# One hybrid decoder layer on one core: three products of TensorE move within the token mixer's step

## What is computed

```python
m = jnp.where(strict, jnp.einsum("bnhid,bnhjd->bnhij", k_beta, k) * decay, 0.0)
sol = lax.linalg.triangular_solve(m, rhs, left_side=True, lower=True, unit_diagonal=True)
attn_intra = jnp.einsum("bnhid,bnhjd->bnhij", q, k) * decay
...
v_new = u_i - jnp.einsum("bhck,bhkv->bhcv", w_i, state)
o = jnp.einsum("bhck,bhkv->bhcv", q_i, state) + jnp.einsum("bhij,bhjv->bhiv", a_i, v_new)
state = state * cd_i[..., None, None] + jnp.einsum("bhck,bhcv->bhkv", k_i, v_new)
```

```python
o = o_inter + jnp.einsum("bhts,bhsv->bhtv", scores, v_i)
state = jnp.exp(last[:, :, 0, :])[..., None] * state + jnp.einsum("bhsk,bhsv->bhkv", k_i * jnp.exp(last - bcum), v_i)
```

## Time and profile before

| | us |
|---|---|
| median of 3 runs | 1436.95 |
| lowest and highest | 1436.75, 1437.14 |
| the profiled execution: its time | 1437.29 |
| its span in the trace | 1435.4 |
| PE busy in the span | 1395.5 (97%) |
| DVE, ACT, POOL busy | 737.5, 542.2, 616.1 |

### The profile page before, as it was taken

How to read it: one execution, slowest core, us unless ns; L and a number is a source line. 1 busy time by engine, 2 the same in 40 slices (tenths; PEclk the granted TensorE clock), 3 DMA queues, 4 the chain that set the end, 5 groups by cost and what they waited for, 6 DMA issues and landing times.

```text
span 1435.4 us, 24659 instructions
## 1 busy us (share of the span) xinstructions
PE 1395.5 (97%) x9457; PEld 1169.4 (81%) x9457; DVE 737.5 (51%) x1288; ACT 542.2 (38%) x1293; POOL 616.1 (43%) x552
## 2 busy tenths in 40 slices
PE   5999999999999999999999999999999999999997
PEld 4777888988888888887887788888888888888886
DVE  5014645465464788884148744543445434444436
ACT  6235445444433455442143423324233242332335
POOL 3234223242334667650303934536345363453650
PEclk9999999999999999999999999999999999999999
DMA  5131313233134324414300112021120211202103
GB/s 178 33 100 49 114 47 119 79 101 107 47 109 123 119 74 129 133 47 151 86 3 0 50 43 84 30 59 60 34 84 30 59 59 32 86 30 59 60 32 130
DMA packets 122003, 106.52 MB, mean 74 GB/s; under 512 B 6352, under 2 KB 107296, under 8 KB 121888
## 3 DMA queue, kind: packets, MB, share of 16 engines
q1 hardware_dynamic: 121744, 104.43, 23.8%
q10 hardware_dynamic: 144, 0.52, 0.2%
HBM read 83.95 MB, written 20.99 MB: 73 GB/s over the span
## 4 chain that ended last, share of the span: by engine, by line
PE 91%; DVE 4%; POOL 2%; issue 2%; ACT 1%; DMA 1%; DVEq 0%; POOLq 0%; ACTq 0%
PE banks L2291 9%; PE banks L2292 9%; PE banks L2293 9%; PE banks L326 6%; PE banks L328 6%; PE banks L327 6%; PE banks L2308 5%; PE banks L2310 5%; PE banks L2309 5%; PE banks L660 2%; PE banks L661 2%; PE banks L662 2%; PE banks L2077 2%; PE banks L2079 2%; PE banks L2078 2%
## 5 line engine op out<-in xcount | busy, mean ns | idle before, releaser
L2415 POOL TENSOR_TENSOR w_l<-area,w_h 128x512 fp32r<-128x512 f32 x102 | 143.4, 1411 | 195.8 <-ACT w_h L2328 195.8
L2415 POOL TENSOR_TENSOR w_l<-w_raw,w_h 128x512 fp32r<-128x512 f32 x86 | 118.1, 1377 | 165.4 <-ACT w_h L2328 165.4
L2559 DVE TENSOR_TENSOR area<-area,banks 128x512 f32<-128x512 f32 x176 | 120.9, 687 | 120.7 <-PE banks L2310 118.3
L326 PE MATMUL banks<-act_h,w_h 128*128 128x512 f32 x352 | 141.3, 401 | 0.0
L328 PE MATMUL banks<-act_h,w_l 128*128 128x512 f32 x352 | 137.5, 391 | 0.0
L327 PE MATMUL banks<-act_l,w_h 128*128 128x512 f32 x352 | 137.3, 390 | 0.0
L2291 PE MATMUL banks<-act_h,w_h 128*128 128x512 f32 x320 | 124.5, 389 | 0.0
L2292 PE MATMUL banks<-act_l,w_h 128*128 128x512 f32 x320 | 124.5, 389 | 0.0
L2308 PE MATMUL banks<-w_h,ff_h 128*128 128x512 f32 x320 | 124.5, 389 | 0.0
L2309 PE MATMUL banks<-w_l,ff_h 128*128 128x512 f32 x320 | 124.5, 389 | 0.0
L2310 PE MATMUL banks<-w_h,ff_l 128*128 128x512 f32 x320 | 124.5, 389 | 0.0
(11 more groups left out here) (303 smaller groups left out, 3302.9 us busy)
## 6 DMA issues: line engine op xcount, KB each, us to landing
w_raw<-in_w_in SPq DMA_DIRECT2D x22, 512.0 KB, 4.0
area<-in_x SPq DMA_DIRECT2D x8, 1024.0 KB, 8.2
projected_tm<-area SPq DMA_DIRECT2D x32, 256.0 KB, 2.4
w_raw<-in_w_gate SPq DMA_DIRECT2D x12, 512.0 KB, 4.6
area<-in_w_down SPq DMA_DIRECT2D x12, 512.0 KB, 4.0
w_raw<-in_w_up SPq DMA_DIRECT2D x12, 512.0 KB, 4.6
projected_cm<-area SPq DMA_DIRECT2D x20, 256.0 KB, 2.3
area<-projected_tm SPq DMA_DIRECT2D x8, 640.0 KB, 5.5
```

Source lines behind the costliest of these rows:

```text
L326: e.matmul(dst, w_h[:, b, k], act_h[:, k, cols], start=(k == 0), stop=False)
L2415: e.tensor_tensor(slot(w_l, u), raw_use(u), slot(w_h, u).bitcast(F32), ALU.subtract).then_inc(sems["fl"], 1)
L2559: e.tensor_tensor(dst, dst, bank(4 + (16 * p + c) % 4), ALU.add).then_inc(sems["x_added"], 1)
```

## The change

Three edits in PE's `step(t)`; no instruction is added, taken away or altered, and the other engines' lists stay as they are. `query_state(t)` goes from behind `pack(u,2)` to right behind `key_state(t)`. `mix_turn(s,0)` goes from behind `update(u,2)` to ahead of it, in the place that `query_state(t)` left. `key_key(v)` goes ahead of `gated_state(t)`.

```diff
@@ -1362,6 +1362,7 @@
                 s, u, v = (t - 1, t + 1, t + 2)
                 if live(t):
                     key_state(t)
+                    query_state(t)
                 if live(u):
                     pack(u, 1)
                     turn(u, 0)
@@ -1376,12 +1377,10 @@
                 if live(u):
                     turn(u, 1)
                     pack(u, 2)
-                if live(t):
-                    query_state(t)
-                if live(u):
-                    update(u, 2)
                 if live(s):
                     mix_turn(s, 0)
+                if live(u):
+                    update(u, 2)
                 if live(u):
                     pack(u, 3)
                 if t == NT:
@@ -1422,10 +1421,10 @@
                 if live(u):
                     pack(u, 6)
                     turn(u, 5)
+                if live(v):
+                    key_key(v)
                 if live(t, NT - 1):
                     gated_state(t)
-                if live(v):
-                    key_key(v)
                 if live(t):
                     gated_out(t)
                 if live(v):
```

More of the change, by code:

```diff
@@ L1378, in step @@
                     pack(u, 2)
-                if live(t):
-                    query_state(t)
+                if live(s):
+                    mix_turn(s, 0)
                 if live(u):
                     update(u, 2)
-                if live(s):
-                    mix_turn(s, 0)
                 if live(u):
```

## The result

The changed kernel took 1443.98 us in the median of 20 runs, the kernel before 1437.61 in 20 runs beside it: ratio 1.0048, 95% interval 1.0037 to 1.0059. The medians lie 6.4 us apart where I had forecast 2.2, and the time is outside my range. Those of before lie between 1436.68 and 1440.16. Those of the changed kernel come in groups: 1436.3 to 1437.9 (3 runs), 1442.3 to 1444.4 (10 runs), 1446.7 to 1449.4 (5 runs), 1453.7 and 1454.0 (2 runs). So something seems to cost several microseconds each time it happens, and to happen never, once or more often in a run.

What follows compares the result with a forecast made beforehand. PE, busy 97% of the span, was taken as the bound, waiting about 1.05 us per 26.60 us step. 3.84 + 2.34 - 2.71 - 0.43 - 0.83 = +2.2 us on 1436.95 gave 1439.1 us, range 1437.0 to 1440.9.

Steps and rivals of the forecast that it cites:

- The waits: PE, mixer loop: none ahead of `pack(u,1)`, about 0.39 us ahead of `pack(u,3)`, about 1.15 (0.74 in step 2) before `key_key`.
- no POOL wait for L1245: POOL, middle of its step: its 1.06 us wait for `query_state` goes, and its `spread` operations end a microsecond sooner.
- Two prices: PE's moved products at old length: `gated_state` 0.64 us onto the path in six steps, `query_state` 1.09 us.
- (0.64 + 0.39) x 4 - 0.65 - 0.37 - 0.65 - 0.19: Steps 2 to 5: `gated_state` 0.64 and new gap 0.39 us each, less filled waits ahead of `update(v,0)`.
- is done about 0.7 us sooner: Step 6: POOL, without 1.59 us of waiting, ends about 0.7 us sooner, so DVE's `final_sb` no longer waits.
- slower beyond that: Rival: POOL still holds `final_sb` in step 6, and step 2 may lose 0.41 us more; 1440.4 us, chance 0.22.
- the rule on exclusive ports: Two-input SBUF operations of DVE meeting earlier POOL work would be longer by up to one POOL operation.
- -0.83 us: Step 6: with `final_sb` free, PE's 0.83 us delay falls into its old wait; bounds 0 and -0.89.
- the wait of 0.89: Step 6: PE's old wait for DVE ahead of `update(u,5)`, forecast to be gone.
- full clock in all 40 slices: Whole span, from the profile page: PE at full clock, so a new order can only win or add waits.

Runs made afterwards that it cites:

- no06: Changed kernel with steps 0 and 6 back in the old order of `query_state`; `key_key` still ahead of `gated_state`: 1438.23 us, ratio 1.0005 to before.
- no06_12: Changed kernel with `query_state` in old order in steps 0 and 6, and `key_key` back behind `gated_state` throughout: 1435.33 us, ratio 0.9989 to before.
- no6: Changed kernel with step 6 alone back in the old order of `query_state`: 1444.67 us, ratio 1.0033 to before.
- only0: Kernel before, with only `query_state` of step 0 moved behind `key_state`: 1436.16 us, ratio 0.9999 to before.
- pool6: Changed kernel plus one POOL wait in step 6, holding its decayed queries until PE's `update(u,2)` is done: 1440.30 us, ratio 1.0029 to before.
- no0: Changed kernel with step 0 alone back in the old order of `query_state`: 1444.73 us, ratio 1.0049 to before.
- e12: Changed kernel with `key_key` put back behind `gated_state`, both other moves kept: 1447.69 us, ratio 1.0061 to before.
- only6: Kernel before, with the `query_state` and `mix_turn` moves in step 6 alone: 1440.96 us, ratio 1.0021 to before.

## Why the prediction was wrong, point by point

**The waits** came as forecast up to step 5. Nothing ahead of `pack(u,1)`; 0.39 ahead of `pack(u,3)`; 1.15 us, and 0.74 in step 2, ahead of `key_key`, but none in step 0, where PE ran at half clock; no POOL wait for L1245. None of them explains the result.

**Two prices were too high.** I took the moved products at their old length, 0.64 and 1.09 us. The chain of after:

```profile
547.94 0.45 PE banks L1319 x4
...
552.78 0.89 PE banks L1245 x8
```

A full-size product right behind another of its shape costs 0.20 (L1245) and 0.19 us (L1319) less. In steps 2 to 5 I had, counted between the starts of `key_key`, (0.64 + 0.39) x 4 - 0.65 - 0.37 - 0.65 - 0.19 = 2.26 us. Less 4 x 0.39 that is 0.70; the rows above give 0.68. The mechanism was right and the size of two terms was off. Over the whole sum they come to 6 x 0.19 for edit 3 and 7 x 0.20 for `query_state` in steps 0 to 6, so the forecast would have been 2.2 - 2.5 = -0.3 us. The runs bear out edit 3's: 6 x 0.45 = 2.7 us, and no06 lies 2.9 above no06_12. This error alone pointed towards faster, away from what was measured.

**Step 6 is the step that failed.** I wrote that POOL "is done about 0.7 us sooner", so that `final_sb` goes free and 0.83 us fall away. That much held: counted from `key_key`, POOL's last operation ended 20.04 us later, against 20.90 before. But I only asked whether POOL's end clears `final_sb`, not what its new beginning meets. Its gates now started before `queries(7,0)`, an operation that I had not looked at, and the run of four held it for 3.50 us. I had named the mechanism, in the rival "slower beyond that" and under the rule on exclusive ports. But I had bounded its price by one POOL operation. The trace shows a DVE operation held across four in a row. In the terms of the sum: I had -0.83 us, with the wait of 0.89 all but gone; PE waited 1.68 instead, so by the waits alone the term is too low by some 1.6 us, and the fall of the clock behind it comes on top. The Trainium skill says that the loser is blocked for the whole instruction (SBUF — State Buffer, "Who interferes with whom"); it does not speak of several in a row, and here the measurement goes further for `queries(7,0)`, while `queries(7,1)` of before was held for one.

**The clock I left out.** I read "full clock in all 40 slices" as a property of the kernel, and said of the range that it held all likely error. The sum had the clock at nothing, without a reason. It depends on the order of the work in single steps: it fell behind the 1.7 us wait of step 6 and in the thin stretch of step 0, and a long fall cost about 7 us (the distance of the two clusters of no6), more than any term of mine. The page's row was not even the full story for before: with its slices of 36 us it cannot show that the clock was at half from 782.2 to 785.6 us, in the feed-forward part, behind a wait of PE of 2.09 us. A window view over the whole span would have told me that this program loses its clock behind a wait. The Trainium skill describes that gate (TensorE: Matmul & The Clock Gate, "Part 1: The HAM clock gate"): two levels, by PE's recent activity. The traces here show the two levels, 0.50 and 1.00, and falls behind waits or thin stretches; which activity decides they do not show. I had the page and no term for it: PE was 97% busy, and I asked what each wait costs, not what it may set off. `query_state` in its old place in step 0 was cover for a level, and with it there no run shows that fall.

**The median** then follows, as I read the groups: with no long fall the change is at 1436.3 to 1437.9, not 1439.1; with one near 1444; with two near 1450 and more. Only one execution, with two long falls, was profiled, so the number of falls in the others is inferred from their times and mean clocks.

## What to carry to other kernels

A full-sized product among small ones may do two jobs, covering a hand-over and helping to keep TensorE's clock up. Before moving it out, look at what PE does for the few microseconds around its old place, in every step of the loop, the first and the last above all. An engine that is freed early is not free of cost: list what it will now run beside. And when a handful of runs scatter by several microseconds, take the runs' own distribution and the clock of each before reasoning about the median. Read the clock in windows of a few microseconds: a row of coarse slices hides short falls.

## What the runs showed of the hardware that I had not expected

- The clock fell to half although PE was "busy" by the timeline through most of the stretch ahead. In step 0 of only0 the two waits just ahead of it were of 0.39 us. It stayed low for 20.5 and 17.1 us in the change, and for 3.4 us in other places (pool6 behind step 6, before at 782.2).
- A fall does not come in every run: the same program had none in some runs and one or more in others (only0: 2 of 12; no6: 7 of 12, by their times).
- A DVE operation with two SBUF operands that had to wait for POOL waited through four POOL operations in a row (3.50 us in after and no0, 3.52 in e12 and only6). Before, another such operation was held for one only (0.85 us).
- The same four-head product cost 0.89 us behind one of its own shape, 1.09 behind small ones.
